# Inverse roots as Sqrt on ScalarE and a reciprocal on VectorE, instead of Ln and Exp on ScalarE

## What is computed

```python
def rms_norm(x, g):
    y = xf * lax.rsqrt(jnp.mean(xf * xf, axis=-1, keepdims=True) + EPS)
    return (y * g).astype(x.dtype)

def layer_norm(x, g, b):                       # on the conv branch, 256 wide
    y = (xf - mu) * lax.rsqrt(var + EPS)

def first_block(...):
    h = rms_norm(x, g_mix) * (1.0 + sc1) + sh1             # norm 0
    x = x + gt1 * token_mix(h, ...)                        # layer_norm; rms_norm of 4 GLA heads
    h = rms_norm(x, g_ffn) * (1.0 + sc2) + sh2             # norm 1
    x = x + gt2 * hier_moe(h, ...)
    return rms_norm(x, g_final)                            # norm 2

def second_block(x, ...):
    for l in range(2):
        x = x + 0.5 * swiglu(rms_norm_2(x, ffn1_norm[l]), ...)
        z = rms_norm_2(x, mix_norm[l]) @ w_in[l]
        qa, ka, va, qs, ks_, vs, zg = jnp.split(z, splits, axis=-1)
        qa = rms_norm_2(qa.reshape(B, S, 8, 64), na_q_norm[l])    # per head, ka and qs alike
        ks_ = rms_norm_2(ks_.reshape(B, S, 2, 64), sw_k_norm[l])
        o_na = neighbourhood_attention(qa, ka, va, na_rpb[l])     # softmax over windows
        o_sw = sliding_window_gqa(qs, ks_, vs, t5_bias, sw_sink[l])
        merged = gate0 * (o_na @ w_branch_na[l]) + gate1 * (o_sw @ w_branch_sw[l])
        x = x + merged @ w_out[l]
        x = x + 0.5 * swiglu(rms_norm_2(x, ffn2_norm[l]), ...)
```

## Time and profile before

| | |
|---|---|
| median of 3 executions | 3120.78 us (3119.65 to 3127.26) |
| the profiled execution | 3127.26 us |
| its span, first to last instruction | 3125.3 us |
| mean granted clock of PE | 0.954 of full speed |
| PE busy | 91% of the span |
| DVE busy | 62% |
| ACT busy | 47% |
| POOL busy | 7% |

### The profile page before, as it was taken

One profiled execution on the slowest core, in us unless ns is written; L12 is line 12 of the kernel. 1 busy time (PEld: TensorE's weight loads), 2 busy tenths in 40 slices (PEclk: granted clock), 3 DMA queues, 4 the chain that ended last, 5 costly groups with the idle time before them and its releaser, 6 DMA issues.

```text
span 3125.3 us, 46845 instructions
## 1 busy us (share of the span) xinstructions
PE 2854.9 (91%) x16210; PEld 2432.9 (78%) x16210; DVE 1934.6 (62%) x2807; ACT 1464.1 (47%) x2192; POOL 233.5 (7%) x116
## 2 busy tenths in 40 slices
PE   5889869998599998997999999999989989999999
PEld 3755657777499986776879998899877767789987
DVE  7542258787599753443369975899553442479964
ACT  3241337776455433553345543655334553355532
POOL 2430200111000002110000000000002110000000
PEclk8997869999799999998999999999999999999999
DMA  7710239997222232111323223223232112322222
GB/s 288 272 41 1 94 138 338 352 356 300 102 103 99 90 112 107 42 40 41 108 87 107 102 97 110 78 100 108 84 99 100 41 34 68 108 95 104 98 88 101
DMA packets 95235, 377.43 MB, mean 121 GB/s; under 512 B 10833, under 2 KB 11105, under 8 KB 92897
## 3 DMA queue, kind: packets, MB, share of 16 engines
q1 hardware_dynamic: 89072, 348.69, 31.4%
q0 software_dynamic: 4608, 16.78, 1.3%
q10 hardware_dynamic: 1456, 10.66, 0.9%
HBM read 363.50 MB, written 16.78 MB: 122 GB/s over the span
## 4 chain that ended last, share of the span: by engine, by line
PE 73%; issue 9%; DVE 8%; ACT 5%; DMA 4%; POOL 2%; ACTq 0%; SPq 0%; DVEq 0%; POOLq 0%
PE pb L1288 12%; PE pb L1289 11%; PE pb L1290 11%; PE pb L1617 9%; PE pb L1619 9%; PE pb L1618 9%; DMA rows<-h_rows,h_idx 3%; PE pb L1813 2%; PE pb L1784 2%; PE pb L1361 1%; POOL w_lo L555 1%; PE pb L1797 1%; DVE SP L2573 1%; ACT SP L1184 1%; PE pb L1607 1%
## 5 line engine op out<-in xcount | busy, mean ns | idle before, releaser
L1617 PE MATMUL pb<-bl,g_wh 128*128 128x256 f32 x2464 | 703.2, 285 | 30.0 <-DVE bl L2351 14.4
L1618 PE MATMUL pb<-bh,g_wl 128*128 128x256 f32 x2464 | 699.1, 284 | 0.0
L1619 PE MATMUL pb<-bh,g_wh 128*128 128x256 f32 x2464 | 699.0, 284 | 0.0
L1617 PEld LDWEIGHTS pb<-bl,g_wh 128*128 128x128 f32 x2464 | 474.8, 193 | 35.0 <-issue 24.1
L1618 PEld LDWEIGHTS pb<-bh,g_wl 128*128 128x128 f32 x2464 | 474.8, 193 | 1.8 <-issue 1.7
L1619 PEld LDWEIGHTS pb<-bh,g_wh 128*128 128x128 f32 x2464 | 474.9, 193 | 0.0
L1288 PE MATMUL pb<-hl,w_hi 128*128 128x512 f32 (+1 forms) x688 | 284.2, 413 | 47.2 <-DVE hl L1911 19.7
L555 POOL TENSOR_TENSOR w_lo<-raw,w_hi 128x1024 fp32r<-128x1024 f32 x72 | 179.5, 2495 | 1949.0 <-ACT w_hi L622 1949.0
L622 ACT ACTIVATE w_hi<-raw 128x1024 fp32r<-128x1024 f32 x196 | 206.1, 1054 | 229.7 <-PE pb L1290 204.9
L1290 PE MATMUL pb<-hh,w_hi 128*128 128x512 f32 (+1 forms) x688 | 273.4, 397 | 0.0
L1289 PE MATMUL pb<-hh,w_lo 128*128 128x512 f32 (+1 forms) x688 | 273.3, 397 | 0.0
(11 more groups left out here) (418 smaller groups left out, 5451.0 us busy)
## 6 DMA issues: line engine op xcount, KB each, us to landing
raw<-in_wstream SPq DMA_DIRECT2D x220, 512.0 KB, 3.5
m_raw<-in_moe_stream SPq DMA_DIRECT2D x192, 512.0 KB, 6.5
g_own<-in_gu_stream SPq DMA_DIRECT2D x44, 768.0 KB, 4.2
raw<-in_gu_stream SPq DMA_DIRECT2D x44, 768.0 KB, 4.2
ada_ring<-in_ada SPq DMA_DIRECT2D x8, 2048.0 KB, 8.5
g_own<-in_gu_stream SPq DMA_DIRECT2D x44, 256.0 KB, 3.0
hidf<-in_gu_stream SPq DMA_DIRECT2D x44, 256.0 KB, 3.0
adaw<-in_ada SPq DMA_DIRECT2D x4, 2048.0 KB, 23.2
```

What stands on the lines that cost most here:

```text
L1617: pe.matmul(o, lh, rl, start=first and k == 0, stop=False, skip_group_check=True)
L1618: pe.matmul(o, ll, rh, start=False, stop=False, skip_group_check=True)
L1619: m = pe.matmul(o, lh, rh, start=False, stop=k == 3, skip_group_check=True)
```

## The change

Ln becomes Sqrt with the same scale and epsilon, and the Exp is dropped. In its place DVE runs `reciprocal` on the whole tile, in front of the multiplication that uses it. The semaphore `rs_ready` (`qk_rs`) is now raised by DVE itself. The five preloads of the set of Ln and Exp in the first block and ahead of the FFN are gone, and the three ahead of the attention and of the norms load Sqrt's table instead. The attention's Exp stays on ACT, so a table is loaded wherever a Sqrt follows an Exp or the other way round. Last, `normed_q` moves on DVE: it stood between `scores(2)` and the remainder of the neighbourhood output, and now stands between `scores(3)` and `normed(3)`.

```diff
@@ ACT: norms
-            def inverse_root(q):
-                act.activation(root[:], pb[0][:], ACT.Ln, scale=1.0 / D, bias=V("eps")).then_inc(root_ready, 1)
-                act.wait_ge(root_ready, q + 1)
-                act.activation(rs[:], root[:], ACT.Exp, scale=-0.5).then_inc(rs_ready, 1)
-
             def norm_root(q):
                 act.wait_ge(stat_mm, 8 * (q + 1))
-                inverse_root(q)
+                act.activation(root[:], pb[0][:], ACT.Sqrt, scale=1.0 / D, bias=V("eps")).then_inc(root_ready, 1)
...
-            act.preload_act_table_set(LN_EXP)
@@ ACT: GLA heads (for h in range(GH))
-                step(act.activation(mt[0:DV, M_OSQ[h], :], pb[B_RMS[h]][0:DV, :], ACT.Ln, scale=1.0 / DV, bias=V("eps")[0:DV]))
-                act.activation(mt[0:DV, M_OSQ[h], :], mt[0:DV, M_OSQ[h], :], ACT.Exp, scale=-0.5).then_inc(o_root, 1)
+                act.activation(mt[0:DV, M_OSQ[h], :], pb[B_RMS[h]][0:DV, :], ACT.Sqrt, scale=1.0 / DV,
+                               bias=V("eps")[0:DV]).then_inc(o_root, 1)
@@ ACT: layer norm
-            act.activation(root[:], pb[0][:], ACT.Ln, scale=1.0 / CONV_W, bias=V("eps")).then_inc(ln_act, 1)
-            act.wait_ge(ln_act, 2)
-            act.activation(rs[:], root[:], ACT.Exp, scale=-0.5).then_inc(ln_act, 1)
+            act.activation(root[:], pb[0][:], ACT.Sqrt, scale=1.0 / CONV_W, bias=V("eps")).then_inc(ln_act, 1)
@@ ACT: ahead of the attention's norm, of FFN 2 and of the next layer
-                act.preload_act_table_set(LN_EXP)
+                act.preload_act_table(ACT.Sqrt)
@@ ACT: root_of of the attention
-                    act.activation(to, pb[bank][:], ACT.Ln, scale=1 / 64, bias=V("eps")).then_inc(qk_root, 1)
-                    act.wait_ge(qk_root, n)
-                    act.activation(to, to, ACT.Exp, scale=-0.5).then_inc(qk_rs, 1)
+                    act.activation(to, pb[bank][:], ACT.Sqrt, scale=1 / 64, bias=V("eps")).then_inc(qk_root, 1)
@@ DVE: norms
+            def norm_rs(q):
+                dve.wait_ge(root_ready, q + 1)
+                dve.reciprocal(rs[:], root[:]).then_inc(rs_ready, 1)
+
             def norm_h(q, hq, gain, shift=None):
+                norm_rs(q)
                 dve.wait_ge(rs_ready, q + 1)
@@ DVE: GLA heads, layer norm, FFN
+                step(dve.reciprocal(o, o))
                 step(dve.scalar_tensor_tensor(o, pb[B_O[h]][0:DV, :], V("gla_g", h)[0:DV], o, ALU.mult, ALU.mult))
...
-            dve.wait_ge(ln_act, 3)
+            dve.wait_ge(ln_act, 2)
+            step(dve.reciprocal(rs[:], root[:]))
...
             def rs_of_norm(n):
+                dve.wait_ge(root_ready, 3 + n + 1)
+                dve.reciprocal(rs[:], root[:]).then_inc(rs_ready, 1)
                 dve.wait_ge(rs_ready, 3 + n + 1)
@@ DVE: attention
                 def qk(n, gained, r, dest, bank_perm):
+                    dve.wait_ge(qk_root, n)
                     dve.wait_ge(qk_gain, n)
+                    dve.reciprocal(r, r).then_inc(qk_rs, 1)
                     dve.wait_ge(qk_rs, n)
...
                     scores(2)
-                    if not last:
-                        normed_q(nq + 3)
                     dve.wait_ge(o_hi, 2 * J + 1)
                     remainder(j, pb[7][:], True).then_inc(o_lo, 1)
                     normed(2)
                     scores(3)
+                    if not last:
+                        normed_q(nq + 3)
                     normed(3)
```

More of the change, by code:

```diff
@@ L116 @@
 N_CHUNKS = C_L + NL * N_LAYER
-LN_EXP = "natural_log_exp_and_others"
 M_OSQ, B_O, B_RMS = (7, 8, 9, 14), (5, 6, 1, 2), (0, 3, 4, 0)
@@ L901, in root_of_norm @@
                 act.wait_ge(stat_mm, STATS[n + 1])
-                inverse_root(3 + n)
-            act.preload_act_table_set(LN_EXP)
+                act.activation(root[:], pb[0][:], ACT.Sqrt, scale=1.0 / D, bias=V("eps")).then_inc(root_ready, 1)
             squares(2, lambda k: act.wait_ge(moe_done, 1), root_ring)
@@ L2087, in _ @@
                                          ALU.mult, ALU.add).then_inc(x_ready, 1)
+            norm_rs(1)
             dve.wait_ge(rs_ready, 2)
@@ L2336, in _ @@
             lo_s31(0, 0)
+            norm_rs(2)
             dve.wait_ge(rs_ready, 3)
```

## The result

The changed kernel takes 3182.7 us (median of 4 executions, 3180.28 to 3183.4), the kernel before 3120.8: a ratio of 1.0192, 95% interval 1.0179 to 1.0204. That is 62 us slower. The forecast was slower by 35.6 us, 3156, with a range up to 3180. The direction was right and the time lies outside the range.

A forecast was written before the change was run, and what follows sets the result against it. PE, busy 91% of the span, was taken as the bound, so ACT or DVE work costs only where PE waits. Terms summed to 31.6 us, with the clock 35.6, on the median 3120.8: 3156.4 us, range 3130 to 3180.

The forecast's parts named there:

- The price of the reciprocal: On DVE at 512 columns: 3.23 us, carried from 175 ns at 3 columns and 181 at 4; ends 0.53 and 4.25.
- The rivals at 0.6, 1.7 and 4.25 us: Reciprocal at plain rate: 3123 us, chance 0.13; midway: 3133, chance 0.10; slower still: 3174, chance 0.14.
- The table loads: On ACT: 33 more of 1.28 us, running ahead of their waits; rival, loads behind their waits: 18 us, 3174, chance 0.07.
- The bare chains: Where a whole stage waits for one root, each loses 2.60 us, reciprocal against Exp; with the other terms 31.6 us.
- prologues: The attention's prologue, twice: 2.2 us at the first root, 2.6 at kn's, less 0.95 beside POOL: 7.7 us.
- FFN entries: Four entries into the FFN: a whole reciprocal enters a DVE chain PE waits for, 2.5 and 3 x 2.1: 8.8 us.
- norm 0 and softplus: First block: norm 0's reciprocal, partly won back, 1.6 us; one more table load before GLA's softplus sigmoids, 0.7 us.
- The loop over pairs, six iterations: 0: Loop over pairs of heads: sn, qn and kn each fit with 0.7 to 1.1 us to spare, so no cost.
- The signs named in the prediction: Included reciprocals near 3.2 us, 33 more loads, longer PE waits, none for sn, qn, kn, and an unchanged loop iteration.
- The clock term: New waits at the FFN's four entries may halve PE's clock behind them: half of 4 x 2.15, 4 us.
- The rival at 3174: Slower reciprocal, 4.25 us: 13.8 us more in bare chains, 3.6 from the loop's overrun spare; chance 0.14.
- The rival of the freed Exps: All 35 dropped Exps outside GLA, 0.63 us each, give 22 us if the reciprocal cost nothing; chance 0.03.

The follow-up runs named there:

- after_short_pool: The changed kernel with POOL subtracting only the first of eight column blocks of each low half in the layers: 3160.2 us, ratio 1.0120.
- attention_only: The kernel before with the change in the attention's 26 roots alone (Sqrt and reciprocal, normed_q behind scores(3)): 3150.0 us, ratio 1.0084.
- after_warm2: The changed kernel with idle matmuls sized to PE's longer waits at norm 2, attention norms, prologues, last pairs and w_out: 3177.0 us, ratio 1.0168.
- qn_back: The changed kernel with normed_q put back behind scores(2): 3195.0 us, ratio 1.0227.
- before_warm: The kernel before with idle matmuls put into waits of PE, 24 of them at norm 2: 3138.6 us, ratio 1.0052.

## Why the prediction was off

- **The price of the reciprocal** was right: 3.35 us measured, 3.23 taken from two rows that differ by one column. The rivals at 0.6, 1.7 and 4.25 us fall. With them fall the two estimates made from pages of the Trainium skill: eight passes, 4.3 us ("VectorE: DVE Perf Modes", section "First, the fixed hardware budget"), is too much, and one pass ("Vector Engine (DVE) Microarchitecture Reference", section 3.2) too little.
- **The table loads** run ahead of their wait, 1.28 us each, with 0.3 us of idle time in front of sixteen of them together; with 33 reciprocals taken out and all loads left, 50 us of the 62 are gone. That rival falls too.
- **The bare chains** came out term by term. PE's added waits against those forecast: layer norm 2.7 (2.6), norm 1 1.0 (0.9), norm 2 4.1 (4.1), attention norms 5.4 (5.2), prologues 7.3 (7.7), FFN entries 7.4 (8.8), norm 0 and softplus 1.7 to 2.0 (2.3), by how much later PE comes to the layer norm. Together some 30 for 31.6.
- **The failed step is "The loop over pairs, six iterations: 0".** Of the added waits, this is the term that was put at nothing and was not. It placed the reciprocal of `qn` ahead of `normed(3)` and gave `normed(3)` its old duration, 1.27 us. POOL was reckoned with for `kn` only. The reciprocal pushes `normed(3)` into the very subtraction of POOL that `kn` used to meet, where it takes 3.37 us, and there the spare of 1 us isn't enough: 1.33 us in each of six iterations, 7.9. `after_short_pool` shows that this is the cause. The signs named in the prediction did not look for it: PE waits for none of `sn`, `qn` and `kn`, but the iteration is longer, 50.5 us for 49.1.
- **The clock term was mis-sized**: 4 us forecast, 20 to 22 measured, as PE's added busy time in the stages with new or longer waits (over the whole kernel it is 14 or 24, by the trace of before that it is held against, since the first block's changes from one execution to the next). I took half of the four FFN entries. All four are at the lower clock now (0.50 over 4.4 us at the first, where it was 1.00) and cost 6.9. So are the first scores behind each prologue (3.78 us for the eight matmuls, 1.99 in the loop) and the third iteration's values (4.53, 2.40 in the second iteration), where waits of 1.32 and 1.45 us follow each other closely. None of these last was in the sum. That filling a wait brings the clock back was shown at places of the kernel before and in the changed kernel's prologue, not at the FFN's entries.
- The two errors, 7.9 and 16 to 18 us, less the 2 us by which the bare chains came out cheaper, make 22 to 24 of the missing 26. The rest is not placed; it is of the size by which two traces of one kernel differ in the first block.
- The rival at 3174 was nearest in time, and it had the loop's spare overrun, but for another reason: its reciprocal of 4.25 us was not there. The rival of the freed Exps counts 35 roots outside GLA; there are 36, which changes nothing.

What stays open is when the clock falls. In both layers of the changed kernel and of `attention_only` it is in the third iteration and not in the first two, which have the same waits; in the second layer of `after_warm2` it is in the second. The FFN's first entry has the same wait of 3.38 us in `after_short_pool`, and its matmuls run at the full clock there.

## What to carry to other kernels

When an instruction is pushed back on DVE, look at what POOL does at its new place as well as at its old one: here 2.1 us of stretching came from a neighbour that had been 1 us away. Price a new wait of PE twice, once as the wait and once as the matmuls behind it, some of which may run at half the clock. Idle matmuls that end before the awaited event won 14 us in the kernel before; a batch of five placed where PE does not wait costs its own 4.5 us. Small forms of an operation already in a trace gave the slope of the large one within 4%.

## What the runs showed of the hardware

A reciprocal on DVE takes 175 ns at 3 columns and 3352 at 512, six times a plain pass of 532 ns. A multiplication of DVE (`tensor_scalar`, 128x256, in place) that starts beside a running POOL subtraction ends only 0.15 us behind it: that makes 3.37 us of 1.27 for four of them in the changed kernel, and 3.13 in `qn_back`. A `tensor_tensor` of two SBUF tiles is held too (2.81 us for 0.68, L2401 in the kernel before). Two other kinds aren't. The six `scalar_tensor_tensor` of `scores(3)`, which read a PSUM bank, take their 1.81 us beside POOL (from 1354.49, POOL from 1354.20 to 1356.60). And a reciprocal isn't either: in the changed kernel's prologue two of them overlap POOL and take their plain 3.35 us (DVE, then POOL):

```profile
1253.59 3.35 DVE L2527 RECIPROCAL root<-root 128x512 f32<-128x512 f32 x1 [5.00 <-ACT root L1112]
...
1263.66 3.35 DVE L2527 RECIPROCAL rs<-rs 128x512 f32<-128x512 f32 x1 [5.99 <-ACT rs L1112]
...
1250.88 4.67 POOL L554 TENSOR_TENSOR w_lo<-raw,w_hi 128x1024 fp32r<-128x1024 f32 x2 [11.30 <-ACT w_hi L621]
1263.13 2.35 POOL L554 TENSOR_TENSOR w_lo<-raw,w_hi 128x1024 fp32r<-128x1024 f32 x1 [7.58 <-ACT w_hi L621]
```

An fp32 idle matmul of 128x512 stood in the trace as two records and took 0.86 us (24 of them: 48 records, 20.8 us, in `before_warm`).
